# A streaming encoder layer on one core: the threshold searches of the last two tiles are moved from the indexer stage into the attention stage

## The chip, the cores and the metric

The kernel runs on one core of a Trainium2 chip, as one program with no host work between its stages. The metric is device time in microseconds (us) of that core, from start to end of the program. TensorE (PE) does the matmuls, VectorE (DVE), ScalarE (ACT) and GpSimd (POOL) the rest; SyncE (SP) issues the DMAs in one fixed order.

## What is computed

One hybrid layer over a prompt of 4096 positions and a sample of 8 x 16 positions, width 1024. All data are fp32.

```
h = rms_norm(x) ; qa,ka,va,ga, qb,kb,vb,gb, qi,ki,wi = split(h @ w_in)     # 2884 columns
A: 8 heads (2 key heads of 64), window of 128 keys + own chunk of 64, relative bias, sinks
B: score[t,s] = sum_h wi[t,h] * relu(qi[t,h] . ki[s])                      # 4 indexer heads
   keep the 256 highest admissible s for each t (lax.top_k)
   softmax over the kept keys of q.k/8 + bias, 8 heads (2 key heads of 64)
y = x + concat(oA * silu(ga), oB * silu(gb)) @ w_out
```

The kernel does not gather. It finds for each row the value of the 256th highest score, makes a mask of that (0 or -2^100), and B attends densely with the mask added to its scores.

## The kernel before

The prompt is cut into 32 tiles of 128 positions (`TILES`), the sample is tile 32. Tile `t` attends to `(t+1)*128` keys. There are three stages, each a block of its own with its own buffers; a stage starts when every engine has finished the one before.

**Stage one (`stage_one`)** projects, norms and transposes q and k, and scores the indexer for each tile: TensorE's products (L584) go through a relu on ScalarE (L707) and are weighted and added on GpSimd (L876, L878, L881) into a score row; a small memset on GpSimd (L885) marks the row ready. Three row buffers go round. Then each row's threshold is searched: 32 tests (`TESTS`), each a count over the whole row. Even tiles are searched by ScalarE (`search`, L766 and L777, with small steps on L781 and L750 between the tests), odd ones by VectorE (L1009). VectorE closes both kinds: it counts once more for even tiles (L959), then makes the mask with L935, L936, a running sum (L938) and two more passes (L943, L946). SyncE stores the mask to DRAM (`store_chosen`, L421 and L422, tensor `chosen`). An order written out by hand in planned times (`us_at`, `ACT_AT`, `DVE_AT`, `FOUND_AT`, `MASK_AT`) places all other work of ScalarE and VectorE between the tests. Two gate blocks of ten early tiles are projected late, in steps 23 to 32 (`LATER`).

**Stage two (`stage_two`)** does the attention. Each tile has six jobs: `k` = 0, 1 are A (four heads each, two steps), `k` = 2 to 5 are B (two heads each, one step for every 512 keys, so `(t+1)/4` rounded up). TensorE's order in a step is: transpose the exponentiated rows of two heads (`turn`, L1516), apply the step before to the values (`apply`, L1545), then score a unit of a later job (`score`, L1491 for A, L1500 for B). ScalarE copies the transposed block of the first head out of PSUM (L1627), then runs exponentials of a coming job (L1606, up to 1024 keys at once). VectorE copies the second head's block (L1759), then adds mask or bias to the new scores and takes the maximum (L1700). There is one PSUM bank of transposes for each head, so a `turn` waits for the copies of the step before, and two slots of scores.

B's scores are made of split operands in a 32-bit format that TensorE takes in one go (`F32R`): GpSimd makes a rounded part and a remainder of q (L1456, L1458), ScalarE and VectorE do the like for the keys (L1582, L1654), in quarters at the start of tiles 0 to 3. A score unit of 512 keys is then four matmuls, two for each head, with 128 partitions and 512 columns. A's scores (L1491) are plain fp32: 64 partitions, 256 columns, the two key heads in the two halves of the partitions.

At the start of stage two a bias table goes through DRAM (`ramp`, L1414, and `table`, L1418), and the first A job waits for it. **The last stage** projects the output and does the sample.

Of the kernel before, what the change touches and what calls it, by code (L numbers as in the profile page):

```python
# [93 lines left out]
def build(nc, x_prompt, x_sample, cache_a_k, cache_a_v, cache_b_k, cache_b_v, cache_b_kidx,  # L94
          norm_g, w_in, q_norm_a, k_norm_a, q_norm_b, k_norm_b, sink_a, rel_bias, w_out,
          one_hot, eye, outs):
    (y_prompt, y_sample, a_k_prompt, a_v_prompt, b_k_prompt, b_v_prompt, b_kidx_prompt,
     a_k_sample, a_v_sample, b_k_sample, b_v_sample, b_kidx_sample) = outs

    def scratch(name, shape, dt=F32):  # L100
        return nc.dram_tensor(name, shape, dt, kind="Internal").ap()


    qk_t = scratch("qk_t", (TILES + 1, P, T_COLS))
    gates = scratch("gates", (TILES + 1, P, D_MODEL))
# [5 lines left out]
    ramp = scratch("ramp", (P, 2 * HEADS, RAMP))  # L111
    stage_one(nc, x_prompt, x_sample, norm_g, w_in, q_norm_a, k_norm_a, q_norm_b, k_norm_b,
              eye, qk_t, gates, values, chosen, qi_new, ki_new, wi_new,
              a_k_prompt, a_v_prompt, b_k_prompt, b_v_prompt, b_kidx_prompt,
              a_k_sample, a_v_sample, b_k_sample, b_v_sample, b_kidx_sample)
    mixed = scratch("mixed", (TILES, P, D_MODEL))
    stage_two(nc, rel_bias, sink_a, one_hot, eye, qk_t, gates, values, chosen, ramp, mixed, a_k_prompt, a_v_prompt)
    stage_last(nc, x_prompt, x_sample, w_out, mixed, cache_a_k, cache_a_v, cache_b_k, cache_b_v, cache_b_kidx, rel_bias, sink_a, eye,
               qk_t, gates, values, qi_new, ki_new, wi_new, chosen, ramp, y_prompt, y_sample, a_k_sample, a_v_sample)
# [8 lines left out]
TESTS = 32  # L128

# [82 lines left out]
def step_us(t):  # L212

    if t > TILES + 1:
        return 100.0
    a = min(max(t - 2, 2), TILES - 1)
    act = 16 * test_us(a // 2 * 2) + sum(act_us(t, s) for s in range(SLOTS))
    dve = 16 * test_us(a // 2 * 2 + 1) + (close_us(a // 2 * 2) + close_us(a // 2 * 2 + 1)) / 2 + sum(dve_us(t, s) for s in range(SLOTS))
    return max(8.5 * len(groups_of_step(t) if t <= TILES else ()) + 8.0 + 4.0 * len(units(max(t - 1, 0))), act, dve)
# [11 lines left out]
def search_times(first, load, extra):  # L231
# [3 lines left out]
    for a in range(first, TILES, 2):  # L235
# [22 lines left out]
for _a in range(2, TILES):  # L258
# [20 lines left out]
def stage_one(nc, x_prompt, x_sample, norm_g, w_in, q_norm_a, k_norm_a, q_norm_b, k_norm_b,  # L279
              eye, qk_t, gates, values, chosen, qi_new, ki_new, wi_new,  # L280
              a_k_prompt, a_v_prompt, b_k_prompt, b_v_prompt, b_kidx_prompt,
              a_k_sample, a_v_sample, b_k_sample, b_v_sample, b_kidx_sample):
    with ExitStack() as ctx:
# [77 lines left out]
        s_last = sem("sample_stored")  # L361
        s_act = sem("act_ticks")
# [9 lines left out]
        def _(sp):  # L372
# [53 lines left out]
            def chosen_until(us):  # L426

                while stored[0] < TILES and MASK_AT[stored[0]] <= us:
# [78 lines left out]
            sp.wait_ge(s_ch, 16 * 2 * (TILES - 2))  # L507
# [103 lines left out]
        def _(act):  # L611
# [213 lines left out]
            for a in range(2, TILES, 2):  # L825
# [72 lines left out]
        def _(dve):  # L898
# [71 lines left out]
            def background():  # L970

                taken = 2
                for t in range(TILES + 5):
                    for slot in (0, 3, 6, 9, 11):
                        while taken < TILES and FOUND_AT[taken] <= us_at(t, slot):
# [11 lines left out]
                while taken < TILES:  # L987
# [38 lines left out]
            for a in range(3, TILES, 2):  # L1026
# [115 lines left out]
def b_head(k, h):  # L1142

    return 2 * (k - 2) + h
# [115 lines left out]

def exps_of_job(n):
# [9 lines left out]
def stage_two(nc, rel_bias, sink_a, one_hot, eye, qk_t, gates, values, chosen, ramp, mixed, a_k_prompt, a_v_prompt):  # L1271
    with ExitStack() as ctx:
# [9 lines left out]
        kT = sb("kT", [P, KVH, SEQ], F32R)  # L1282
        v = sb("v", [P, TILES, P])
        qa = sb("qa", [P, GROUP, P])
        q_raw = sb("q_raw", [P, HEADS, P])
        q_part = [sb(f"q_part_{i}", [P, 2, HEADS, P], F32R) for i in range(2)]
# [5 lines left out]
        pT = [[sb(f"pT_{h}_{i}", [P, STEP]) for i in range(2)] for h in range(2)]  # L1292
        gate = sb("gate2", [P, D_MODEL])
# [28 lines left out]
        s_khi = sem("keys_rounded")  # L1322
        s_klo = sem("keys_split")
# [3 lines left out]
        s_qr = sem("qb_loaded")  # L1327
# [4 lines left out]
        s_split = sem("q_split")  # L1332
# [16 lines left out]
        s_pool = sem("pool_ticks2")  # L1349
# [3 lines left out]
        def _(sp):  # L1353
# [6 lines left out]
            def load_keys(i):  # L1360

                many = PART // P
                for vh in range(KVH):
                    for half in range(2):
                        sp.dma_start(row[vh][half * HD:(half + 1) * HD, 1, i * PART:(i + 1) * PART].rearrange("p (o n) -> p o n", n=P),
                                     qk_t[i * many:(i + 1) * many, vh * HD:(vh + 1) * HD, 9 * P:10 * P].rearrange("o p n -> p o n")).then_inc(s_kraw[i], 16)
# [6 lines left out]

            sp.wait_ge(s_zero, 1)
# [10 lines left out]
            def load_q(t):  # L1385
                if t:
                    sp.wait_ge(s_split, t)
                for half in range(KVH):
                    rows = slice(half * HD, (half + 1) * HD)
                    sp.dma_start(q_raw[rows, :, :].rearrange("p (v g) n -> p v (g n)", v=KVH),  # L1390
                                 qk_t[t, :, 4 * P:8 * P].rearrange("(v d) n -> d v n", v=KVH)).then_inc(s_qr, 16)
# [9 lines left out]
            def load_mask(t):  # L1401
# [3 lines left out]
                sp.wait_ge(s_near, t - 1)  # L1405
                sp.dma_start(mask[t % 2][:, 0:near], chosen[t, :, 0:near]).then_inc(s_m[t % 2], 16)
# [22 lines left out]
            sp.dma_start(a_v_prompt[0, 0].rearrange("t h d -> t (h d)"), values[TILES - 1, :, 0:P]).then_inc(s_win, 16)  # L1429
            for t in range(TILES + 1):  # L1430
                if t >= 1:
                    sp.wait_ge(s_used, mixed_by(t - 1, 1))
                    sp.dma_start(mixed[t - 1, :, STEP:2 * STEP], mixT[1][:, :]).then_inc(s_store[1], 16)
                if t == TILES:
# [16 lines left out]
        def _(pool):  # L1451
            for t in range(TILES):
                pool.wait_ge(s_qr, 32 * (t + 1))
                if t >= 2:
                    pool.wait_ge(s_unit, units_through(6 * t - 7))
                pool.tensor_copy(q_part[t % 2][:, 0], q_raw[:, :, :]).then_inc(s_pool, 1)  # L1456
                pool.wait_ge(s_pool, t + 1)
                pool.tensor_tensor(q_part[t % 2][:, 1], q_raw[:, :, :], q_part[t % 2][:, 0].bitcast(F32), ALU.subtract).then_inc(s_split, 1)  # L1458
# [12 lines left out]
        def _(pe):  # L1471
# [4 lines left out]
            def score(n, j):  # L1476
# [99 lines left out]
        def _(act):  # L1576
            def round_keys(i):

                act.wait_ge(s_kraw[i], 16 * 2 * KVH)
                cols = slice(i * PART, (i + 1) * PART)  # L1580
                for vh in range(KVH):
                    act.activation(kT[:, vh, cols], row[vh][:, 1, cols], ACT.Copy).then_inc(s_khi, 1)  # L1582

            round_keys(0)

# [29 lines left out]

            for x in PLAN["first"]:
                exponential(*x)
            for n in range(N_JOBS):
                if n % 6 == 0 and 1 <= n // 6 < PARTS:
                    round_keys(n // 6)  # L1620
                for g in range(n_steps(n)):
# [8 lines left out]
                    for kind, m, j in PLACED[n, g]:  # L1630
                        if kind == "gate":
                            copy_gate(m, j)
            copy_gate(TILES - 1, 1)

        @block.vector
        def _(dve):
# [11 lines left out]
            def split_keys(i):  # L1648

                cols = slice(i * PART, (i + 1) * PART)  # L1650
                for vh in range(KVH):
                    dve.wait_ge(s_khi, KVH * i + vh + 1)
                    low = kT[HD:P, vh, cols]
                    dve.tensor_tensor(low, row[vh][HD:P, 1, cols], low.bitcast(F32), ALU.subtract).then_inc(s_klo, 1)  # L1654

            split_keys(0)
# [85 lines left out]

            use(0, 0)
            use(1, 0)
            for n in range(N_JOBS):
                t, k = divmod(n, 6)
                if k == 0 and 1 <= t < PARTS:
                    split_keys(t)
# [4 lines left out]
                for g in range(n_steps(n)):  # L1753
# [592 lines left out]
```

## Time and profile before

| what | value |
|---|---|
| median of 3 runs | 5419.87 us (5418.57 to 5422.72) |
| the profiled execution, its time | 5422.48 us |
| its span, first to last instruction | 5420.7 us |
| PE busy over the span | 4360.3 us (80%), 24457 matmuls |
| DVE busy | 3629.5 us (67%) |
| ACT busy | 3253.0 us (60%) |
| POOL busy | 1729.3 us (32%) |
| mean granted TensorE clock | 0.895 |

The span lies 1.8 us inside the profiled execution's time, and that time is 2.6 us above the median. A busy share is a mean over three stages with different limits, so it has to be read stage by stage. A row of the timeline gives the start in us, the duration, the engine, the line, and how many instructions were merged; what follows an arrow is what ended the wait before it.

### The profile page before, as it was taken

To read this page: it belongs to the slowest core of one execution; us is meant where nothing else is said; L and a number is where in the kernel's file an instruction comes from. 1 tells how busy PE (TensorE), PEld (TensorE's weight loads), DVE (VectorE), ACT (ScalarE), POOL (GpSimd) and SP (SyncE) were. 2 spreads that over 40 slices of the span, in tenths; PEclk is the share of its full clock that TensorE was granted. 3 is DMA by queue.
4 is the path that set the end of the run, shared out by engine and by line. 5 is a ranking of instruction groups with operands and counts; after the bars stand their busy time and mean duration, and the time that the engine had idled before them with its cause. 6 is when DMAs were issued, how large, how long until landed. Compare 5 with 4: busy or idle time off the path is not lost. (4 is left out here: it accounts for less than half of the span.)

```text
span 5420.7 us, 73770 instructions
## 1 busy us (share of the span) xinstructions
PE 4360.3 (80%) x24457; PEld 2782.8 (51%) x24457; DVE 3629.5 (67%) x6737; ACT 3253.0 (60%) x6235; POOL 1729.3 (32%) x1384
## 2 busy tenths in 40 slices
PE   6777777776678777762078899999999999989999
PEld 3434444433334334331046677777777777765454
DVE  2457778888879989898667666666666666635111
ACT  1689788888788789776055555555555555530100
POOL 1454566675758657761022111110000000000000
PEclk9888888888788888886579999999999999999999
DMA  5111111100011011000252111111010100033422
GB/s 133 52 45 41 39 37 38 34 33 33 25 46 39 31 46 38 32 26 31 47 134 71 51 47 43 39 42 43 27 41 28 42 24 28 27 101 121 123 96 99
DMA packets 210852, 280.99 MB, mean 52 GB/s; under 512 B 51200, under 2 KB 139232, under 8 KB 210464
## 3 DMA queue, kind: packets, MB, share of 16 engines
q1 hardware_dynamic: 207520, 276.10, 17.0%
q8 instruction: 204, 3.34, 0.3%
q14 instruction: 168, 1.38, 0.1%
q10 hardware_dynamic: 2960, 0.17, 0.0%
HBM read 165.15 MB, written 112.10 MB: 51 GB/s over the span
## 5 line engine op out<-in xcount | busy, mean ns | idle before, releaser
L1009 DVE TENSOR_SCALAR_CACHE_REDUCE ties<-score,cand 128x512 int8<-128x512 f32 (+14 forms) x480 | 1253.7, 2612 | 141.7 <-POOL score L885 125.3
L568 PE MATMUL bank<-w,x 128*128 128x512 f32 (+1 forms) x2848 | 1241.7, 591 | 25.4 <-DVE w L907 12.6
L777 ACT ACTIVATE act_junk<-score,a_cand,a_sign 128x384 int8<-128x384 f32 (+14 forms) x450 | 990.2, 2201 | 15.0
L1700 DVE CUSTOM_DVE_ANT_0 row<-bank,mask 128x512 f32<-128x512 f32 (+3 forms) x1024 | 623.0, 639 | 465.2 <-PE bank L1500 465.1
L568 PEld LDWEIGHTS bank<-w,x 128*128 128x128 f32 x2848 | 570.0, 204 | 605.1 <-issue 535.0
L1627 ACT ACTIVATE pT<-bank 128x512 f32<-128x512 f32 (+2 forms) x704 | 370.4, 526 | 772.8 <-PE bank L1516 771.9
L584 PE MATMUL bank<-kiT,qi 128*128 128x512 f32 (+3 forms) x1136 | 397.3, 493 | 421.9 <-ACT relu L707 219.7
L1500 PE MATMUL bank<-kT,q_part 128*128 128x512 f32 (+3 forms) x2304 | 658.8, 408 | 11.2 <-DVE part L1700 7.1
L1606 ACT ACTIVATE row<-row,top 128x1024 f32<-128x1024 f32 (+7 forms) x640 | 633.2, 991 | 5.1 <-DVE top L1713 5.0
L1516 PE MATMUL bank<-ident,row 128*128 128x128 f32 x4224 | 574.5, 276 | 52.1 <-DVE pT L1759 48.0
L1545 PE MATMUL bank<-pT,v 128*64 128x128 f32 x8448 | 595.2, 282 | 0.0
L881 POOL TENSOR_TENSOR score<-score,relu 128x512 f32<-128x512 f32 (+3 forms) x426 | 572.8, 1345 | 33.4
L1516 PEld LDWEIGHTS bank<-ident,row 128*128 128x128 f32 x4224 | 497.2, 142 | 134.6 <-DVE pT L1759 54.8
L584 PEld LDWEIGHTS bank<-kiT,qi 128*128 128x128 f32 x1136 | 239.2, 233 | 554.9 <-ACT relu L707 289.6
L878 POOL TENSOR_TENSOR relu<-relu,weight 128x512 f32<-128x512 f32 (+3 forms) x426 | 505.7, 1187 | 0.0
L1545 PEld LDWEIGHTS bank<-pT,v 128*64 128x64 f32 x8448 | 454.4, 137 | 97.7 <-issue 97.4
L1759 DVE COPY pT<-bank 128x512 f32<-128x512 f32 (+2 forms) x704 | 422.9, 601 | 118.0 <-PE bank L1516 116.8
L1456 POOL CAST q_part<-q_raw 128x1024 fp32r<-128x1024 f32 x32 | 33.2, 1038 | 1385.2 <-DMA q_raw<-qk_t 1385.2
L1500 PEld LDWEIGHTS bank<-kT,q_part 128*128 128x128 f32 x2304 | 383.8, 191 | 166.3 <-issue 96.5
L707 ACT ACTIVATE relu<-bank 128x512 f32<-128x512 f32 (+3 forms) x568 | 296.2, 560 | 263.1 <-POOL score L881 177.9
L2102 PE MATMUL bank<-wo,mix_in 128*128 128x512 f32 x1024 | 448.7, 597 | 0.0
L876 POOL TENSOR_TENSOR score<-relu,weight 128x512 f32<-128x512 f32 (+3 forms) x142 | 154.6, 1089 | 765.6 <-issue 553.7
(215 smaller groups left out, 4774.8 us busy)
## 6 DMA issues: line engine op xcount, KB each, us to landing
qk_t<-ring SPq DMA_DIRECT2D x66, 256.0 KB, 2.0
gates<-ring SPq DMA_DIRECT2D x66, 256.0 KB, 2.0
gate<-gates SPq DMA_DIRECT2D x33, 512.0 KB, 3.5
out<-x_in SPq DMA_DIRECT2D x33, 512.0 KB, 2.9
x<-in_x_prompt SPq DMA_DIRECT2D x32, 512.0 KB, 3.7
q_raw<-qk_t SPq DMA_DIRECT2D x64, 256.0 KB, 5.8
mixed<-mixT SPq DMA_DIRECT2D x64, 256.0 KB, 2.1
mix_in<-mixed SPq DMA_DIRECT2D x32, 512.0 KB, 4.3
```

Source lines behind the costliest of these rows:

```text
L568: ins = pe.matmul(p_bank[n % 2][:, 0:n1 - n0], held[:, c * P:(c + 1) * P], w[:, c, n0:n1], start=(c == 0), stop=(c == KC - 1))
L584: ins = pe.matmul(s_bank[at % 4][:, 0:n], qi[:, part, h * P:(h + 1) * P], kiT[:, c:c + n], start=(part == 0), stop=(part == 1))
L777: tick(act.activation(junk, row, ACT.Sign, bias=c, scale=back, accum_out=a_sum[:, :]))
L878: k = tick(pool.tensor_tensor(r, r, weighs, ALU.mult))
L881: pool.tensor_tensor(to, to, r, ALU.add).then_inc(s_pa, 1)
L1009: n = tick(dve.tensor_scalar(ties[:, 0:width], row, c.bitcast(F32), 0.0, ALU.is_ge, ALU.add, accum_out=counts[:, i:i + 1]))
L1500: ins = pe.matmul(s[:, h * STEP:h * STEP + w], q_part[t % 2][:, i, head, :], kT[:, head // GROUP, c:c + w], start=(i == 0), stop=(i == 1))
L1516: ins = pe.transpose(t_bank[h][:, b * P:(b + 1) * P], held, ident[:, :])
L1545: ins = pe.matmul(oT[0 if k < 2 else 1][half * HD:(half + 1) * HD, col:col + P], value, pT[h][at % 2][:, b * P:(b + 1) * P], start=first, ...
L1606: act.activation(at, at, ACT.Exp, bias=bias, accum_out=out).then_inc(s_exp, 1)
L1700: ins = dve.tensor_tensor_reduce(row[k % 2][:, h, c0:c0 + w0], s[:, h * STEP + c0 - c:h * STEP + c0 - c + w0], more, 1.0, PAD, ALU.add, AL ...
L2102: ins = pe.matmul(y_bank[k % 2], held, w[:, c, i * STEP:(i + 1) * STEP], start=(c == 0), stop=(c == KC - 1))
```

## The change

Two things change with it, and a third follows from the room in memory.

1. Stage one searches only tiles 2 to 29 (`SEARCHED` = 30). The finished score rows of tiles 30 and 31 are stored to DRAM (`late`, 128 x 4096 fp32 each, of which 3968 and 4096 columns are used) at the end of SyncE's list, and the stage's end waits for them.
2. Stage two loads row 30 at its start and row 31 at the start of tile 20. ScalarE searches them in pieces placed behind its other work of a B step: 161 pieces over the 208 B steps of tiles 3 to 18, and 161 over the 240 of tiles 20 to 28. VectorE closes them in 23 pieces each, in the B steps of tiles 19 and 29. A test is now four counts over 1024 columns each (the last 896 for tile 30) and one piece of small operations. The masks of tiles 30 and 31 go from a buffer to the mask buffers by DMA.
3. B's scores are no longer split. q and k stay plain fp32 with the two key heads in the two halves of the partitions, a job pairs one head of each half (`b_head`), and a unit of 512 keys is four matmuls of 64 partitions and 256 columns. The casts and subtractions on L1456, L1458, L1582 and L1654 go, and the keys are loaded once (one DMA for a quarter instead of four) and q in one DMA instead of two.

```diff
+SEARCHED = TILES - 2
+LATE_TILES = tuple(range(SEARCHED, TILES))
...
@@ stage_one, sync
+            for a in LATE_TILES:
+                sp.wait_ge(s_sum, a - 1)
+                sp.dma_start(late[a - SEARCHED, :, 0:(a + 1) * P], row_of(a)).then_inc(s_late, 16)
...
+            sp.wait_ge(s_late, 16 * len(LATE_TILES))
@@ stage_one, scalar and vector
-            for a in range(2, TILES, 2):
+            for a in range(2, SEARCHED, 2):
                 search(a)
...
-            for a in range(3, TILES, 2):
+            for a in range(3, SEARCHED, 2):
                 search(a)
@@ the plan of stage two
 def b_head(k, h):
-    return 2 * (k - 2) + h
+    return GROUP + (k - 2 ^ 1) if h else k - 2
...
+QUARTER = 1024
+LATE_SPANS = {1: ((3, 27, 28),), 2: ((3, 18, 19), (20, 28, 29))}[len(LATE_TILES)]
...
+for _a, (_first, _last, _close) in zip(LATE_TILES, LATE_SPANS):
+    _steps, _many = wide_steps(_first, _last), TESTS * (len(quarters(_a)) + 1) + 1
+    for _i in range(_many):
+        LATE_ACT[_steps[_i * len(_steps) // _many]] += 1
+    _steps, _many = wide_steps(_close, _close), 2 + 5 * len(quarters(_a)) + 1
+    for _i in range(_many):
+        LATE_DVE[_steps[_i * len(_steps) // _many]] += 1
@@ stage_two, tensor
-                pe.wait_ge(s_split, t + 1)
-                pe.wait_ge(s_klo, KVH * (t * P // PART + 1))
-                for h in range(2):
-                    head = b_head(k, h)
-                    for i in range(2):
-                        ins = pe.matmul(s[:, h * STEP:h * STEP + w], q_part[t % 2][:, i, head, :], kT[:, head // GROUP, c:c + w],
-                                        start=(i == 0), stop=(i == 1))
+                pe.wait_ge(s_qb[t % 2], 16 * (t // 2 + 1))
+                pe.wait_ge(s_kraw[c // PART], 16)
+                for c0 in range(0, w, 2 * P):
+                    m = min(2 * P, w - c0)
+                    for h in range(2):
+                        vh, g = divmod(b_head(k, h), GROUP)
+                        half = slice(vh * HD, (vh + 1) * HD)
+                        ins = pe.matmul(s[:, h * STEP + c0:h * STEP + c0 + m], qb[t % 2][half, g, :], kT[half, c + c0:c + c0 + m],
+                                        start=True, stop=True)
@@ stage_two, scalar
-            round_keys(0)
...
+                    def count(c, scale):
+                        for q, (c0, n) in enumerate(parts):
+                            act.wait_ge(s_lact, late_tick.n)
+                            late_tick(act.activation(late_junk[:, 0:n], late_row[:, c0:c0 + n], ACT.Sign, bias=c, scale=scale,
+                                                     accum_out=l_sums[:, q:q + 1]))
+                            yield
+                        then(l_sums[:, 4:4 + len(parts)], l_sums[:, 0:len(parts)], ACT.Copy, accum_out=l_sum[:, :])
...
                     for kind, m, j in PLACED[n, g]:
                         if kind == "gate":
                             copy_gate(m, j)
+                    for _ in range(LATE_ACT[n, g]):
+                        next(late_work, None)
@@ stage_two, vector (late_close: the closing passes, in quarters but for the running sum)
+                    m = tick(dve.tensor_tensor_scan(row, tie, tie, 0.0, ALU.add, ALU.max))
...
+                    for _ in range(LATE_DVE[n, g]):
+                        next(late_work, None)
```

## Rows read from the trace of the kernel before

**Rows 1.** Windows by stage: PE, PEld, DVE, ACT, POOL busy, clock, DMA share, GB/s
```profile
0.00:2666.00 2666.00, 1834.40 (x5063) 968.71 (x5063) 2088.40 (x2428) 1998.92 (x3318) 1484.40 (x1278) 0.83 0.13 41
2666.00:2725.00 59.00, 3.53 (x18) 1.91 (x18) 10.09 (x15) 3.65 (x5) 6.82 (x5) 0.50 0.91 165
2725.00:4819.00 2094.00, 1953.31 (x17240) 1531.58 (x17240) 1394.78 (x4018) 1206.32 (x2822) 231.59 (x92) 0.96 0.15 43
```

**Rows 2.** Timeline of VectorE at the end of stage one
```profile
2452.53 4.48 DVE L1009 TENSOR_SCALAR_CACHE_REDUCE ties<-score,cand 128x4096 int8<-128x4096 f32 x1 [18.32 <-POOL score L885]
...
2657.37 4.42 DVE L946 SCALAR_TENSOR_TENSOR mask<-ties,mask 128x4096 bf16<-128x4096 int8 x1
```

**Rows 3.** Timeline of SyncE's DMA queue across the change of stage
```profile
2662.24 0.43 SPq L422 DMA_DIRECT2D chosen<-mask  x1
2666.29 0.34 SPq L1354 DMA_DIRECT2D ident<-in_eye  x1
```

**Rows 4.** GpSimd's groups by line from 2357 to 2453 us; timeline of TensorE
```profile
L876 POOL TENSOR_TENSOR score<-relu,weight 128x512 f32<-128x512 f32 x8 | 8.3, 1039 | 36.9 <-issue 28.9 <-ACT relu L707 8.0
...
2447.35 7.03 PE L568 MATMUL bank<-w,x_later 128*128 128x512 f32 x16
```

**Rows 5.** DMA issues by line: KB each, median us from issue to landing
```profile
ramp<-ramp_sb SPq DMA_DIRECT2D x1, 3064.0 KB, 34.0
...
chosen<-mask SPq DMA_DIRECT2D x1, 960.0 KB, 3.7
```

**Rows 6.** Timeline of TensorE in tile 21: an ordinary step of B
```profile
3817.00 1.09 PE L1545 MATMUL bank<-pT,v 128*64 128x128 f32 x16
3818.02 1.21 PE L1500 MATMUL bank<-kT,q_part 128*128 128x512 f32 x4
3819.07 1.04 PE L1516 MATMUL bank<-ident,row 128*128 128x128 f32 x8
```

**Rows 7.** Timeline of TensorE: an A unit, then parts of it in narrow windows
```profile
3823.65 1.13 PE L1491 MATMUL bank<-ka,qa 64*128 64x256 f32 x8
3824.71 0.98 PE L1500 MATMUL bank<-kT,q_part 128*128 128x384 f32 x4
...
3824.18 0.60 PE L1491 MATMUL bank<-ka,qa 64*128 64x256 f32 x4
...
3824.40 0.38 PE L1491 MATMUL bank<-ka,qa 64*128 64x256 f32 x2
```

**Rows 8.** What TensorE waited for, stage two: total us, times, longest
```profile
PE bank L1516 <- DVE pT L1759: 99.1, 57, 3.6
```

**Rows 9.** Windows of tile 17 and tile 28, columns as in rows 1
```profile
3468.00:3540.00 72.00, 67.98 (x583) 53.35 (x582) 46.64 (x132) 40.81 (x99) 7.51 (x3) 0.93 0.13 39
4407.00:4512.00 105.00, 99.72 (x901) 79.14 (x898) 67.99 (x192) 59.02 (x126) 7.52 (x3) 0.98 0.10 31
```

**Rows 10.** ScalarE's count by forms (min/median/max ns), and two tests of tile 30
```profile
L777 ACT ACTIVATE act_junk<-score,a_cand,a_sign x450: 706/2201/3695, 173.0 to 2520.1; 128x384 int8<-128x384 f32 x10, 128x640 int8<-128x640 f32 x10, 128x896 int8<-128x896 f32 x10, 128x1152 int8<-128x1152 f32 x10
...
2506.01 3.69 ACT L777 ACTIVATE act_junk<-score,a_cand,a_sign 128x3968 int8<-128x3968 f32 x1
2510.58 3.69 ACT L777 ACTIVATE act_junk<-score,a_cand,a_sign 128x3968 int8<-128x3968 f32 x1
```

**Rows 11.** ScalarE's groups by line, stage two: busy us, mean ns, idle before
```profile
L1606 ACT ACTIVATE row<-row,top 128x1024 f32<-128x1024 f32 x416 | 473.8, 1141 | 0.0
L1627 ACT ACTIVATE pT<-bank 128x512 f32<-128x512 f32 x480 | 286.4, 597 | 598.5 <-PE bank L1516 598.3
L1606 ACT ACT_TABLE_LOAD x1 | 1.3, 1283 | 0.0
```

**Rows 12.** VectorE: closing passes of tile 31 (timeline), and stage two's scores
```profile
2644.02 8.69 DVE L938 TENSOR_TENSOR_SCAN score<-ties 128x4096 f32<-128x4096 int8 x1
2652.74 4.48 DVE L943 SCALAR_TENSOR_TENSOR ties<-score,pick,ties 128x4096 int8<-128x4096 f32 x1
...
L1700 DVE CUSTOM_DVE_ANT_0 row<-bank,mask 128x512 f32<-128x512 f32 (+3 forms) x1024 | 623.0, 639 | 465.2 <-PE bank L1500 465.1
```

More of the change, by code:

```diff
@@ L111, in build @@
     ramp = scratch("ramp", (P, 2 * HEADS, RAMP))
+    late = scratch("late", (len(LATE_TILES), P, SEQ))
     stage_one(nc, x_prompt, x_sample, norm_g, w_in, q_norm_a, k_norm_a, q_norm_b, k_norm_b,
-              eye, qk_t, gates, values, chosen, qi_new, ki_new, wi_new,
+              eye, qk_t, gates, values, chosen, late, qi_new, ki_new, wi_new,
               a_k_prompt, a_v_prompt, b_k_prompt, b_v_prompt, b_kidx_prompt,
@@ L116, in build @@
     mixed = scratch("mixed", (TILES, P, D_MODEL))
-    stage_two(nc, rel_bias, sink_a, one_hot, eye, qk_t, gates, values, chosen, ramp, mixed, a_k_prompt, a_v_prompt)
+    stage_two(nc, rel_bias, sink_a, one_hot, eye, qk_t, gates, values, chosen, late, ramp, mixed, a_k_prompt, a_v_prompt)
     stage_last(nc, x_prompt, x_sample, w_out, mixed, cache_a_k, cache_a_v, cache_b_k, cache_b_v, cache_b_kidx, rel_bias, sink_a, eye,
@@ L216, in step_us @@
     a = min(max(t - 2, 2), TILES - 1)
+    both = min(a // 2 * 2 + 1, SEARCHED - 1)
     act = 16 * test_us(a // 2 * 2) + sum(act_us(t, s) for s in range(SLOTS))
-    dve = 16 * test_us(a // 2 * 2 + 1) + (close_us(a // 2 * 2) + close_us(a // 2 * 2 + 1)) / 2 + sum(dve_us(t, s) for s in range(SLOTS))
+    dve = 16 * test_us(both) * (both % 2) + (close_us(a // 2 * 2) + close_us(both)) / 2 + sum(dve_us(t, s) for s in range(SLOTS))
     return max(8.5 * len(groups_of_step(t) if t <= TILES else ()) + 8.0 + 4.0 * len(units(max(t - 1, 0))), act, dve)
@@ L234, in search_times @@
     waiting = sorted(extra)
-    for a in range(first, TILES, 2):
+    for a in range(first, SEARCHED, 2):
         ready = us_at(a + 1, 8.7)
@@ L257 @@
 FOUND_AT, MASK_AT = {}, {}
-for _a in range(2, TILES):
+for _a in range(2, SEARCHED):
     if _a % 2 == 0:
@@ L279, in stage_one @@
 def stage_one(nc, x_prompt, x_sample, norm_g, w_in, q_norm_a, k_norm_a, q_norm_b, k_norm_b,
-              eye, qk_t, gates, values, chosen, qi_new, ki_new, wi_new,
+              eye, qk_t, gates, values, chosen, late, qi_new, ki_new, wi_new,
               a_k_prompt, a_v_prompt, b_k_prompt, b_v_prompt, b_kidx_prompt,
@@ L426, in chosen_until @@
             def chosen_until(us):
-                while stored[0] < TILES and MASK_AT[stored[0]] <= us:
+                while stored[0] < SEARCHED and MASK_AT[stored[0]] <= us:
                     store_chosen(stored[0])
@@ L974, in background @@
                     for slot in (0, 3, 6, 9, 11):
-                        while taken < TILES and FOUND_AT[taken] <= us_at(t, slot):
+                        while taken < SEARCHED and FOUND_AT[taken] <= us_at(t, slot):
                             yield FOUND_AT[taken]
@@ L986, in background @@
                 yield FAR_AWAY - 1
-                while taken < TILES:
+                while taken < SEARCHED:
                     choose_act(taken)
@@ L1258, with wide_steps, quarters @@
             EXP_AT[_x] = len(EXP_AT)
+QUARTER = 1024
+LATE_SPANS = {1: ((3, 27, 28),), 2: ((3, 18, 19), (20, 28, 29))}[len(LATE_TILES)]
+def wide_steps(first, last):
+    return [(n, g) for n in range(6 * first, 6 * last + 6) if n % 6 >= 2 for g in range(n_steps(n))]
+def quarters(a):
+    return [(c, min(QUARTER, (a + 1) * P - c)) for c in range(0, (a + 1) * P, QUARTER)]
+LATE_ACT = {_s: 0 for _s in STEP_AT}
+LATE_DVE = {_s: 0 for _s in STEP_AT}
+for _a, (_first, _last, _close) in zip(LATE_TILES, LATE_SPANS):
[5 more added lines that the diff above has]
+        LATE_DVE[_steps[_i * len(_steps) // _many]] += 1
 def exps_of_job(n):
@@ L1268, in exps_for, with stage_two @@
     return EXP_AT["exp", n, a_place(g, h) if n % 6 < 2 else 2 * (g // 2) + h] + 1
-def stage_two(nc, rel_bias, sink_a, one_hot, eye, qk_t, gates, values, chosen, ramp, mixed, a_k_prompt, a_v_prompt):
+def stage_two(nc, rel_bias, sink_a, one_hot, eye, qk_t, gates, values, chosen, late, ramp, mixed, a_k_prompt, a_v_prompt):
     with ExitStack() as ctx:
@@ L1281, in stage_two @@
         near_bias = sb("near_bias", [P, HEADS, NEAR])
-        kT = sb("kT", [P, KVH, SEQ], F32R)
+        kT = sb("kT", [P, SEQ])
         v = sb("v", [P, TILES, P])
         qa = sb("qa", [P, GROUP, P])
-        q_raw = sb("q_raw", [P, HEADS, P])
-        q_part = [sb(f"q_part_{i}", [P, 2, HEADS, P], F32R) for i in range(2)]
+        qb = [sb(f"qb_{i}", [P, GROUP, P]) for i in range(2)]
         ka = sb("ka", [P, 2, P])
@@ L1326, in stage_two @@
         s_qa = sem("qa_loaded")
-        s_qr = sem("qb_loaded")
+        s_qb = [sem(f"qb_loaded_{i}") for i in range(2)]
         s_ka = sem("ka_loaded")
@@ L1362, in load_keys @@
                 many = PART // P
[L1363 to L1366, printed above, removed]
+                sp.dma_start(kT[:, i * PART:(i + 1) * PART].rearrange("p (o n) -> p o n", n=P),
+                             qk_t[i * many:(i + 1) * many, :, 9 * P:10 * P].rearrange("o p n -> p o n")).then_inc(s_kraw[i], 16)
             def load_part(i):
@@ L1385, in load_q @@
             def load_q(t):
[L1386 to L1391, printed above, removed]
+                if t >= 2:
+                    sp.wait_ge(s_unit, units_through(6 * t - 7))
+                sp.dma_start(qb[t % 2][:, :, :], qk_t[t, :, 4 * P:8 * P].rearrange("p (g n) -> p g n", g=GROUP)).then_inc(s_qb[t % 2], 16)
             def load_values(t):
@@ L1405, in load_mask @@
                 sp.wait_ge(s_near, t - 1)
+                if t in LATE_TILES:
+                    sp.wait_ge(s_lmask, LATE_TILES.index(t) + 1)
+                    sp.dma_start(mask[t % 2][:, 0:near], late_mask[:, 0:near]).then_inc(s_m[t % 2], 16)
+                    sp.dma_start(mask[t % 2][:, near:near + NEAR], late_mask[:, near:near + NEAR]).then_inc(s_m[t % 2], 16)
+                    return
                 sp.dma_start(mask[t % 2][:, 0:near], chosen[t, :, 0:near]).then_inc(s_m[t % 2], 16)
@@ L1429, in _, with load_late @@
             sp.dma_start(a_v_prompt[0, 0].rearrange("t h d -> t (h d)"), values[TILES - 1, :, 0:P]).then_inc(s_win, 16)
+            def load_late(i):
+                if i:
+                    sp.wait_ge(s_lmask, i)
+                width = (LATE_TILES[i] + 1) * P
+                sp.dma_start(late_row[:, 0:width], late[i, :, 0:width]).then_inc(s_lrow, 16)
+            load_late(0)
             for t in range(TILES + 1):
@@ L1433, in _ @@
                     sp.dma_start(mixed[t - 1, :, STEP:2 * STEP], mixT[1][:, :]).then_inc(s_store[1], 16)
+                if t in [close + 1 for _, _, close in LATE_SPANS[:-1]]:
+                    load_late([close + 1 for _, _, close in LATE_SPANS].index(t) + 1)
                 if t == TILES:
@@ L1576, in _ @@
         def _(act):
[L1577 to L1582, printed above, removed]
-            round_keys(0)
             def exponential(kind, n, i):
@@ L1632, in _ @@
                             copy_gate(m, j)
+                    for _ in range(LATE_ACT[n, g]):
+                        next(late_work, None)
+            for _ in late_work:
+                pass
             copy_gate(TILES - 1, 1)
@@ L1646, in _ @@
             dve.tensor_copy(ramp_sb[:, :], bank[0:2 * HEADS, 0:383]).then_inc(s_rampc, 1)
[L1648 to L1656, printed above, removed]
             dve.wait_ge(s_tab, 16 * 2)
```

160 lines of the change are left out of this document (144 added, 16 removed).

## The prediction

> **What bounds the kernel now.** I read the windows by stage first, then the timelines at each stage's end, then a step of stage two. Stage one lasts to 2666 us [rows 1]. At its end only the last search is left: GpSimd has row 31 ready at 2452.5, and from there VectorE counts, closes and is done at 2661.8 [rows 2]; the store goes out at 2662.2 and stage two's first DMA at 2666.3 [rows 3]. So some 210 us of the end are one engine's work on tile 31 (and the closing of tile 30). Then 59 us pass with 3.5 us of matmuls, at a granted clock of 0.50 (the 1.2 GHz level), while the bias table goes through DRAM: the `ramp` DMA alone takes 34.0 us [rows 1, 5]. From 2725 to 4819 TensorE is the bound: 1953 of 2094 us busy, with VectorE at 1395 and ScalarE at 1206 [rows 1]. The last stage, 602 us, is not touched, and I leave it as it is.
>
> **Stage one, removed.** Both searches and both closings of tiles 30 and 31 go, but not all of the time from 2452.5 on is theirs. Row 31 itself stays. Its adds had 8.0 us of waits for ScalarE's relus [rows 4], which were queued behind tests of 3.7 us [rows 10]; those tests are gone, so I put the row at 2444.5. The gates' projections that are still queued on TensorE then, four of 7.0 us [rows 4], start at about 2437 and end at 2465; three transposes, their copies and three stores follow, an estimate of 5 us. SyncE then reaches what is new: two stores of 1984 and 2048 KB, issued together. Their price is not in the trace. A store of 960 KB from the same kind of buffer lands in 3.7 us, which makes 8 us the least for 4032 KB at twice its rate and 15.5 at its own; the `ramp` DMA, 3064 KB in 34.0 us, makes 45 the most [rows 5]. The form is that of the mask store (long rows of one buffer), so I take 12. The stage ends near 2482, stage two starts 1 us later, at 2483.5 instead of 2666.3: **-183 us**, bounds -150 and -190.
>
> **Start of stage two.** The `ramp` chain stays. In front of it in the queue, four key loads become one with half the bytes, and two q loads one: **-3**. Rounding and splitting of the keys at the starts of tiles 1 to 3 goes from ScalarE and VectorE, about 2 us each time (two instructions of 1024 columns, of the size of an exponential [rows 11]): **-6**. GpSimd's q casts lay beside everything; going, they give nothing.
>
> **B's scores.** Before, from the first score matmul of a full unit to the next transpose 1.05 us pass (3818.02 to 3819.07) [rows 6]. After, the unit has the form of half an A unit: eight matmuls of 64 x 256 take 1.06 us (3823.65 to 3824.71) [rows 7]. They run in pairs, one in each half of the partitions: the third pair starts at 3824.18, the fourth at 3824.40, so the pitch is 0.22 us for a pair, the first gap is 0.31 (0.53 less one pitch), and from the last pair to the next instruction it is 0.31 [rows 7]. Two pairs therefore take 0.31 + 0.31 = 0.62 to 0.63, not half of 1.06. I take 0.63, a gain of 0.41; the other end is 0.53, a gain of 0.52. Gaps before the first score matmul are in both forms part of the 1.02 of `apply` [rows 6, 7]. There are 480 full units (ScalarE's 480 copies of 512 columns count the same steps [rows 11]) and 96 partial ones of 128, 256 or 384 keys. Full: 480 x 0.41 = 197. Partial ones cost less before as well (0.98 us for 384 keys against 1.21 for 512 [rows 6, 7]) and have one pair or two after; 0.25 is my estimate of their mean gain, 96 x 0.25 = 24. Together 221.
>
> The Trainium skill, TensorEngine Tiling (Array Packing), section Key Properties, says that tiles run in parallel but that a change of tiling mode drains TensorE. Here the change adds one such switch to a step, since scores used to share the full-array form with the transposes. By the first half alone a unit would take 0.53 and the time would be 5070 (480 x 0.11 less); with the gaps of 0.31 that the row shows, which the second half may be the reason of, it is the sum below. The trace agrees as far as the pitch of the pairs goes.
>
> Not all 221 reach the end. TensorE waited 57 times for VectorE's copy, 99.1 us in all [rows 8]: near an A unit VectorE has several us of work in a row, and what TensorE saves just ahead of it comes back as a longer wait. I take off 0.55 us for each, 31, and 6 for tiles 0 to 7, where steps are few and chains of waits count more. **-184**, bounds -150 (twice the loss) and -245 (0.52 a unit, half the loss).
>
> **The searches on ScalarE.** From 384 to 3968 columns a count grows from 706 to 3695 ns [rows 10], 0.834 ns a column, so 1024 columns take 1.24 us; with the reading of the sum, which overlaps half, 1.25 of the engine. A test's small operations take the rest of 4.57 us between two counts, 0.9 [rows 10], and one more copy with a sum: about 1.2. So 322 pieces of 1.25 are 400 us more on ScalarE, of which 1206 were busy [rows 1]. On average it fits. Tile 17: 72 us less 4 x (4 x 0.41 + 0.27) = 64.4, ScalarE 40.8 + 15.5 x 1.25 = 60.2, 93%. Tile 28: 105 less 12.3 = 92.7, ScalarE 59.0 + 21.5 x 1.25 = 85.9, 93% [rows 9]. But ScalarE is not free evenly. A step of B becomes 3.05 - 0.41 = 2.64 us; ScalarE's copy takes 0.5 of it and an exponential of 1024 columns 1.13 (the rows' durations less the overlap with the next) [rows 11], so a step with one late piece needs 2.9 and one with two exponentials 4.0. The copy may be some 1.4 us late before the next `turn` waits: half a `turn` of 1.04 and 0.6 of copy end it some 1.1 us after the `turn` starts [rows 6, 11], and the next starts at 2.64. Job by job, tile 17: ScalarE 2.4 + 5.5 + 3.9 x 1.25 = 12.8, TensorE 4.5 x 2.64 = 11.9, so 0.9 of a job shows, 3.6 of a tile. In the same way tile 10 has 2.4, tile 28 nothing (18.7 against 19.1). Tiles 3 to 18 at a mean of 2.4 make 39, tiles 20 to 28 some 5, and I add 6 for unevenness: **+50**, bounds +10 (TensorE's present waits of 3 us a tile absorb it) and +130 (0.4 of each piece shows). The wait that takes the place of VectorE's is then "transposes for ScalarE's copy L1627".
>
> **The closings on VectorE.** Its B step is two scores at 0.64 and a copy of like size, 1.9 us [rows 12]; with a quarter of a closing pass, 4.48 / 4 = 1.12 [rows 12], it is over 2.64 by some 0.4, in 12 pieces of a closing (the two cheap passes fit). The running sum is not cut: 8.69 us [rows 12], of which 1.4 are hidden. 12 x 0.4 + 7.3 = 12.1, with small operations 13, twice: **+26**, bounds 15 and 45. What is queued behind it on VectorE is its copy, and TensorE's next `turn` waits for that.
>
> **The reload.** Row 31 (2048 KB) is issued at the start of tile 20 ahead of tile 21's loads, which have a whole tile of time; only ScalarE's first piece may wait, **+3**. Waits that are new on SyncE (for the masks) are long past when it gets there. Row 30's load at the start is queued ahead of tile 2's loads, in place of keys that are no longer loaded twice: 0, at most 5.
>
> **Sum.** -183 - 3 - 6 - 184 + 50 + 26 + 3 = -297. The profiled execution's 5422.5 less 297 is 5125.5; it stood 2.6 above the median, so 5123.
>
> **The rivals.**
> - ScalarE binds more than I think: lateness does not heal between jobs, because late pieces stand ahead of the copy for which TensorE waits. At the upper bound, +130, the time is 5203. For it: 93% mean use in both tiles, and exponentials in pairs. Against: TensorE already waits 3 us in each tile.
> - The scores gain nothing: the pairs do not overlap in this place, or the switches eat it. Then -184 goes, and ScalarE has its old 3.05 us step, which saves about 30 of the 50: 5277. Against it stand the A units, which are in the same place of the step.
> - Everything hides and the unit costs 0.53: -245 instead of -184, +10 and +15 instead of +50 and +26, near 5010.
> - Slower: ScalarE has to change its function tables between the searches' sign and the exponentials. Stage two has one table load of 1283 ns now, before its first exponential [rows 11], and that exponential and copy share a table is all that it shows. With a load before and after each of 322 pieces, 826 us are added; ScalarE then has 1206 + 400 + 826 = 2432 us of work in a stage of 2094, and the time is at least 5423 - 183 - 9 + 338 = 5569, with stalls some 5650. It decides from about 115 pieces with a pair of loads, all of them exposed (297 / 2.57). The Trainium skill, ScalarE: Activation LUTs, section on table sets, speaks of this danger (batch calls by set) and prices a switch at 2.66 us, by which it would be twice as bad; it also says that cheap functions are in every set. No row here has sign beside an exponential.
>
> **How the numbers follow.** The sum as taken, within 60 us: 0.60. ScalarE binds: 0.18. Scores gain nothing: 0.07. All hides: 0.11. Tables: 0.04. The range runs from 5030 to 5220: it takes in the likeliest case, the first rival, and the upper bound of the late rows' stores, and leaves out most of the other three. A difference of 0.2% (11 us) is what a measurement of this kernel can tell from none. Only the tables make it slower: faster 0.95, the same 0.01, slower 0.04.
>
> **What would show it.** Stage two's first DMA near 2484; stage one's last wait of SyncE for the stores of late rows, some 12 us. In an ordinary step of a tile without late work (tile 30 or 31) a period of 2.64 instead of 3.05, and score units of four matmuls of 64 x 256 in 0.63. In tiles 3 to 18 waits of L1516 for ScalarE's copy, 2 to 4 us a tile. In tiles 19 and 29 one gap of 7 us behind the running sum. One table load in stage two. The prediction is wrong if the unit takes 0.8 or more, if the waits for ScalarE's copy add up to over 100 us, or if the rows' stores take 30.

## The result, and the profile after

The changed kernel takes 5289.19 us (median of 4 runs, 5285.59 to 5291.09) against 5420.36 before (4 runs): a ratio of 0.9757, 95% interval 0.974 to 0.9774, so 131 us less. The forecast was 5123. The profiled execution has a span of 5286.3 us.

First the windows by stage of the kernel after, columns as in [rows 1]:

```profile
0.00:2481.00 2481.00, 1828.35 (x5063) 968.10 (x5063) 1884.68 (x2277) 1858.14 (x3170) 1485.85 (x1278) 0.86 0.14 45
2481.00:2538.00 57.00, 3.53 (x18) 1.91 (x18) 7.09 (x13) 1.79 (x4) 3.35 (x39) 0.50 0.88 162
2538.00:4687.00 2149.00, 1988.78 (x19288) 1491.53 (x19288) 1445.42 (x4077) 1559.40 (x3622) 127.49 (x31) 0.97 0.12 39
```

Stage one ends 185 us sooner, as forecast. But stage two, which should have lost some 110 us (-184 - 6 + 50 + 26 + 3), has become 55 longer (2149 after 2094), and TensorE is busier in it than before (1988.8 after 1953.3), with 19288 entries after 17240. ScalarE has 353 us more to do there, and that is not where the time went, as TensorE's waits show (total, times, longest):

```profile
PE bank L1577 <- DVE pT L1935: 117.5, 63, 7.3
PE bank L1577 <- ACT pT L1756: 16.8, 35, 1.0
```

It waits 16.8 us in all for ScalarE's copy, and 18 us longer than before for VectorE's [rows 8]. The end of stage one, in SyncE's DMA queue:

```profile
2469.23 0.94 SPq L508 DMA_DIRECT2D late<-score  x2
2481.07 0.34 SPq L1403 DMA_DIRECT2D ident<-in_eye  x1
```

The late rows go out at 2469.2 and stage two's first DMA at 2481.1. So the two stores hold the end of the stage for 12 us, as the forecast took it.

Now an ordinary step of B in tile 17, TensorE's timeline, to be set beside [rows 6]:

```profile
3305.79 1.13 PE L1561 MATMUL bank<-kT,qb 64*128 64x256 f32 x8
3306.86 1.09 PE L1577 MATMUL bank<-ident,row 128*128 128x128 f32 x8
3307.88 1.09 PE L1606 MATMUL bank<-pT,v 128*64 128x128 f32 x16
3308.90 1.13 PE L1561 MATMUL bank<-kT,qb 64*128 64x256 f32 x8
```

The score unit of 512 keys has eight entries, not four, and takes 1.07 us (3305.79 to 3306.86), where the old one took 1.05. The whole step is 3.11 us (3305.79 to 3308.90) against 3.02 (the score unit before the one in [rows 6] starts at 3815.00, that one at 3818.02). The forecast had 0.63 and 2.64. The unit is in every respect what an A unit is in [rows 7], and this is the clue. In the code both have four matmuls. By source line, with number of entries and min/median/max in ns:

```profile
L1561 PE MATMUL bank<-kT,qb x4352: 269/376/793, 2539.1 to 4651.7; 64*128 64x256 f32 x184, 64*128 64x128 f32 x14
```

The program issues 480 x 4 + 32 x (4 + 2 + 2) = 2176 of these matmuls, and the trace has 4352. A plain fp32 matmul is two entries. The old ones, in the split format, were one entry each: 2304 in the profile's page for 576 units of four.

Two windows by tile, for tiles 17 and 28, to be set beside [rows 9]:

```profile
3283.00:3356.00 73.00, 68.50 (x657) 51.28 (x656) 47.05 (x133) 57.78 (x137) 4.09 (x1) 0.95 0.11 35
4255.00:4361.00 106.00, 100.66 (x1012) 75.71 (x1012) 68.33 (x192) 83.03 (x182) 4.09 (x1) 1.00 0.09 28
```

ScalarE has 17 and 24 us more to do in these tiles, and they are 1 us longer each.

### The profile page after: what moved, and what is told of

Same layout as the page of the kernel before. It is cut to its first block and busy times, and to the rows that moved or that the text cites. A ratio compares the mean times of both kernels' runs of the same rounds, so it can differ in the third digit from the quotient of the medians.

```text
span 5286.3 us, 78323 instructions
## 1 busy us (share of the span) xinstructions
PE 4389.2 (83%) x26505; PEld 2741.8 (52%) x26505; DVE 3473.8 (66%) x6644; ACT 3463.7 (66%) x6887; POOL 1623.2 (31%) x1358
## 5 line engine op out<-in xcount | busy, mean ns | idle before, releaser
L1018 DVE TENSOR_SCALAR_CACHE_REDUCE ties<-score,cand 128x512 int8<-128x512 f32 (+13 forms) x448 | 1110.6, 2479 | 122.4 <-POOL score L894 107.1
L786 ACT ACTIVATE act_junk<-score,a_cand,a_sign 128x384 int8<-128x384 f32 (+13 forms) x420 | 879.8, 2095 | 14.0
L1526 POOL TENSOR_TENSOR near_bias<-table,mask 128x2048 f32<-128x2048 f32 (+1 forms) x32 | 129.6, 4050 | 1932.3 <-DVE part L1824 1879.6
L1577 PE MATMUL bank<-ident,row 128*128 128x128 f32 x4224 | 603.2, 283 | 69.5 <-DVE pT L1935 65.4
L1561 PE MATMUL bank<-kT,qb 64*128 64x256 f32 (+1 forms) x4352 | 615.6, 399 | 14.6 <-DVE row_a L1798 7.4
L1577 PEld LDWEIGHTS bank<-ident,row 128*128 128x128 f32 x4224 | 455.6, 142 | 256.2 <-issue 168.6
L1606 PEld LDWEIGHTS bank<-pT,v 128*64 128x64 f32 x8448 | 458.2, 138 | 97.8 <-issue 97.4
L1561 PEld LDWEIGHTS bank<-kT,qb 64*128 64x128 f32 x4352 | 383.1, 189 | 136.6 <-issue 82.5
```

The source lines that it names most:

```text
L786: tick(act.activation(junk, row, ACT.Sign, bias=c, scale=back, accum_out=a_sum[:, :]))
L1018: n = tick(dve.tensor_scalar(ties[:, 0:width], row, c.bitcast(F32), 0.0, ALU.is_ge, ALU.add, accum_out=counts[:, i:i + 1]))
L1561: ins = pe.matmul(s[:, h * STEP + c0:h * STEP + c0 + m], qb[t % 2][half, g, :], kT[half, c + c0:c + c0 + m], start=True, stop=True)
L1577: ins = pe.transpose(t_bank[h][:, b * P:(b + 1) * P], held, ident[:, :])
L1606: ins = pe.matmul(oT[0 if k < 2 else 1][half * HD:(half + 1) * HD, col:col + P], value, pT[h][at % 2][:, b * P:(b + 1) * P], start=first, ...
```

## Experiments

Theory 1: the score unit is no quicker, since its count of matmuls was misread, and is even 0.09 us of a step slower; the late work costs little. Theory 2, the rival: the unit is quicker somewhere, and the late pieces on ScalarE eat what it gains.

**Each part alone.** The first kernel has the new scoring and no late search; the second has the late rows stored and loaded, but neither searched nor closed; the third has ScalarE's pieces and no closings. The second and third leave out the masks of tiles 30 and 31 (all zero), so they give times only.

```diff
@@ first kernel
-SEARCHED = TILES - 2
+SEARCHED = TILES
...
@@ second kernel
-                    for _ in range(LATE_ACT[n, g]):
-                        next(late_work, None)
...
@@ second and third kernel
-                    for _ in range(LATE_DVE[n, g]):
-                        next(late_work, None)
```

> The changed scoring and nothing else: all searches are back in stage one, no late row is stored, loaded or searched. Theory 1 (the new score unit is no quicker: a plain fp32 matmul of the code is two entries of the trace, so an A unit's eight entries are the four matmuls of a whole new unit): a B step is 3.11 us instead of 3.02, 480 steps cost some 43 us, the keys' splitting and the shorter start give back 15, so about 5448. Theory 2 (the unit gains 0.41 as forecast and ScalarE's late pieces eat it in the changed kernel): about 5420 - 184 - 9 = 5227.

> The changed kernel without the pieces on ScalarE and VectorE: the late rows are stored and loaded, never searched or closed, and the masks of tiles 30 and 31 are all zero. Theory 1: stage two loses only the closings, 30 us, and little else: about 5255. Theory 2 (the pieces hide a gain of the scores): about 5289 - 184 - 30 = 5075.

> The changed kernel with ScalarE's 322 pieces, without VectorE's 46 closing pieces (the masks of tiles 30 and 31 are all zero). Against the run without any late work it gives the price of ScalarE's pieces, against the changed kernel that of the closings. Theory 1: closings 29 us, so 5260, and ScalarE's pieces 5 or less, since a step of 3.11 us has room for 2.9. Theory 2: ScalarE's pieces cost over 100 us, closings 29: 5260 too, but then the run without late work is at 5160 or below.

Measured: scores alone 5450.5 against 5420.8 for the kernel before, timed beside it (ratio 1.0054, 1.0037 to 1.007); no late work 5258.7; no closings 5261.1. Theory 1 had 5448, 5255 and 5260. The new scoring makes the kernel slower by itself, by 30 us net of what the keys' splitting gives back. ScalarE's 322 pieces cost 5261.1 - 5258.7 = 2.4 us, less than the scatter of two runs: with the same code in stage one, stage two's first DMA went out at 2477.4 in the second kernel and at 2481.1 in the changed one. VectorE's closings cost 5289.2 - 5261.1 = 28. Theory 2 falls with the first kernel.

**Are the halves used side by side?** The heads of a job are paired as before, so both lie in the same half of the partitions.

```diff
-    return GROUP + (k - 2 ^ 1) if h else k - 2
+    return 2 * (k - 2) + h
```

> The changed kernel with the heads of a job paired as before (both in one half of the partitions), so that no two score matmuls can run side by side. Theory 1: the side-by-side pairs are what keeps the new unit at 1.06 us; without them it takes about 8 x 0.22 + 0.1 = 1.9, and 528 units of 512 keys cost some 440 us more: about 5730. A rival, that the halves do not overlap in this place and the unit is merely cheap, gives no change: 5289.

5652.2 us. TensorE's timeline:

```profile
3503.83 1.99 PE L1561 MATMUL bank<-kT,qb 64*128 64x256 f32 x8
3505.75 1.09 PE L1577 MATMUL bank<-ident,row 128*128 128x128 f32 x8
```

The unit now takes 1.92 us, 0.85 more, so two halves do run side by side in the changed kernel. Full units make 480 x 0.85 = 408 (there are 480, not the 528 of the expectation); 363 arrive. TensorE's waits for VectorE's copy account for 52 us of the difference, since they fall from 117.5 to:

```profile
PE bank L1577 <- DVE pT L1935: 65.2, 55, 6.4
```

That is more than the 45 missing, and the 96 partial units, which must cost more as well, are not in the 408; the rest was not taken apart.

**The form of the unit.** One matmul of 512 columns for each head instead of two of 256, and in another kernel the unit ahead of `apply`.

```diff
-                for c0 in range(0, w, 2 * P):
-                    m = min(2 * P, w - c0)
+                for c0 in range(0, w, 4 * P):
+                    m = min(4 * P, w - c0)
```

> The changed kernel with one matmul of 512 columns for each head of a score unit instead of two of 256. Theory: the unit is bound by the streaming of its columns, in two entries of the trace for each matmul, side by side in two halves, and by a gap of 0.31 us at either end. The columns stay the same, only the first gap can hide behind a longer first matmul: 0.0 to 0.1 us less in 480 steps, 5240 to 5289. A rival, that the number of instructions sets the unit: half the entries, 0.5 us a unit, near 5040.

```diff
                     turn(n, g)
+                    if last is not None and [kind for kind, _, _ in PLACED[n, g]] == ["score"]:
+                        score(*PLACED[n, g][0][1:])
+                        apply(*last)
+                        last = (n, g)
+                        continue
```

> The changed kernel with the score unit of a step in front of the applying of the step before, where a step has one unit and no gate. The number of changes between full-array, halved and column-split matmuls stays three for a step. Theory: 3.11 us of a step against 3.02 come from the entry into and out of the halved form (gaps of 0.31 and 0.17 us beside 0.23 and 0.11), whatever stands next to it: the same, 5280 to 5300; VectorE gets its scores a microsecond earlier, which may take some of the 117 us of waits for its copy.

5290.1 and 5292.8 us: no change in either that stands out from the scatter of the runs. In the first a unit is

```profile
3507.74 1.13 PE L1561 MATMUL bank<-kT,qb 64*128 64x512 f32 x4
3508.80 1.09 PE L1577 MATMUL bank<-ident,row 128*128 128x128 f32 x8
```

1.06 us with half the entries, so the number of matmuls is not what it costs; the columns are, as the half units below confirm. The order of the parts does not matter either.

**If the unit had been what the forecast took it for.** From tile 6 on the second half of each wide unit is left out (its scores are those of an earlier unit), which leaves two pairs of entries side by side, with the late work and, as in the second kernel, without.

```diff
-                for c0 in range(0, w, 2 * P):
+                for c0 in range(0, w if t < 6 else 2 * P, 2 * P):
```

> The changed kernel with the second half of each wide score unit left out from tile 6 on (its scores are those of an earlier unit), so that a unit is two pairs side by side, the form that the forecast priced at 0.63 us. It tests the rest of the forecast. By its steps: 468 x 0.43 + 7 - 31 = 177 less, and with a step of 2.68 us the late pieces on ScalarE cost 50 and not 2: 5289 - 177 + 48 = 5160. If ScalarE still hides all: 5112. If ScalarE binds (0.4 of each piece): 5240.

> The same half units without any late work on ScalarE and VectorE (as in the second experiment; masks of tiles 30 and 31 zero). By the forecast's steps 5259 - 177 = 5082; the run before less this one is the price of the late work at the shorter step, forecast as 76 (50 and 26).

5136.2 and 5097.8 us. The first kernel's step, where the unit takes 0.63 us as the forecast had it for a unit of this size:

```profile
3513.84 0.70 PE L1561 MATMUL bank<-kT,qb 64*128 64x256 f32 x4
3514.47 1.09 PE L1577 MATMUL bank<-ident,row 128*128 128x128 f32 x8
```

Half the unit gives back 153 us with the late work and 161 (5258.7 - 5097.8) without, where the forecast's way of counting gave 177. The late work costs 38 at the shorter step (5136.2 - 5097.8), not the 76 forecast and not the 30 of the longer step (5289.2 - 5258.7). TensorE's waits here:

```profile
PE bank L1577 <- DVE pT L1935: 140.2, 68, 7.7
PE bank L1577 <- ACT pT L1756: 23.8, 44, 2.8
```

Even with a step of 2.68 us ScalarE does not bind. The same two waits in the kernel without late work are 119.0 and 14.3 us, so the late work adds 21 us of waits for VectorE and 10 for ScalarE. The shorter step itself adds 21 for VectorE (97.8 to 119.0, both without late work), which the forecast took at 31. With 21 in place of 31 its count would be 187, and 161 arrive; the missing 26 were not taken apart. The granted clock over stage two is 0.95 without late work at the short step and 0.97 at the long one, which has that sign.

**Two versions that should be faster.** A closing's running sum is cut into eight pieces, and row 30's closing lies over tiles 18 and 19 (ScalarE's pieces then end with tile 17).

```diff
-                    m = tick(dve.tensor_tensor_scan(row, tie, tie, 0.0, ALU.add, ALU.max))
+                    for c in range(0, width, EIGHTH):
+                        n = min(EIGHTH, width - c)
+                        tie = late_tie[:, c:c + n]
+                        dve.wait_ge(s_dve, tick.n)
+                        tick(dve.tensor_tensor_scan(late_row[:, c:c + n], tie, tie, late_row[:, c - 1:c] if c else 0.0, ALU.add, ALU.max))
+                        if c + n < width:
+                            yield
```

> The changed kernel with the running sum of a closing cut into eight pieces of 512 columns that hand the sum on, and row 30's closing spread over tiles 18 and 19 instead of 19 alone. Theory: the closings cost 28 us because one instruction of 8.4 us stands in front of VectorE's copy, and pieces of 1.1 us fill what the step leaves; cut, 18 of the 28 us go: 5271. A rival, that the closing costs by its sum of work on VectorE: no change, 5289, since the work stays the same.

5270.9 us (0.9719, 0.9705 to 0.9734), as expected. The 18 us are the gain of both edits, which were not run apart. What the cut removes is seen in the changed kernel in tile 19, first VectorE, then TensorE:

```profile
3478.54 8.42 DVE L1902 TENSOR_TENSOR_SCAN late_row<-late_tie 128x3968 f32<-128x3968 int8 x1
...
3487.13 0.68 DVE L1935 COPY pT<-bank 128x512 f32<-128x512 f32 x1
```

```profile
3480.17 0.66 PE L1577 MATMUL bank<-ident,row 128*128 128x128 f32 x4
3487.87 1.11 PE L1577 MATMUL bank<-ident,row 128*128 128x128 f32 x4 [7.05 <-DVE pT L1935]
```

The sum takes 8.42 us, the copy behind it starts at 3487.1, and TensorE stands for 7.05; in tile 29 it is 8.69 and 7.31. With the cut sum the longest wait is 3.7 us, and all waits for VectorE's copy make 105.0 us instead of 117.5.

In the other version the late rows are stored inside step 32 of SyncE's list, and the last kernel has both.

```diff
                     from_ring(ki_new, HD, P)
+                    for a in LATE_TILES:
+                        sp.wait_ge(s_sum, a - 1)
+                        sp.dma_start(late[a - SEARCHED, :, 0:(a + 1) * P], row_of(a)).then_inc(s_late, 16)
```

> The changed kernel with the stores of the two late rows issued in step 32, behind the sample's indexer operands, and not at the end of SyncE's list. The 11 us from their issue to stage two's first DMA are then behind the last gates' projections. Theory: 9 us less, 5280. A rival: row 31 is ready too late and its wait holds up the stores behind it: 0 or slower.

> The changed kernel with both, the running sum in pieces and the early stores. They are in different stages and should add: 5289 - 18 - 9 = 5262.

5284.3 us (0.9743, 0.9727 to 0.9759) for the early stores, 5259.8 (0.9702, 0.9687 to 0.9717) for both. In the profiled execution of the early stores stage two starts 12 us sooner (first DMA at 2468.6, not 2481.1), of which 3 were there before the moved stores (the gates' store ahead of them goes out at 2441.7, not 2444.7); the other 9 are what was expected. But the median moved by 5, less than its runs differ (5278.1 to 5288.8). With identical instructions from there on, its tiles 20 to 22 took 6.7 us longer at a granted clock of 0.94 to 0.96 than in the changed kernel at 0.96 to 0.98. So that gain is not shown in the time by itself. The version with both is 29 us below the changed kernel and the best of those that leave nothing out; it is 11 below the cut sum alone, though the runs of the two overlap (5253.8 to 5267.8, and 5264.5 to 5272.3).

## Why the prediction was wrong

It failed at one step, **B's scores**, "the unit has the form of half an A unit: eight matmuls of 64 x 256 take 1.06 us". The row says x8, and the code beside it, two times two matmuls, says four. Each plain fp32 matmul is two entries of the trace, so an A unit is a whole new unit, and [rows 7] already said what a new one costs: 1.06 us from its start to the next instruction, against 1.05. I counted entries on one side (eight for A) and matmuls of the code on the other (four for the new unit). The unit took 1.07 us, over the 0.8 that the prediction named as the sign of being wrong, and the whole gain of 184 was missing. The bounds of the step, 0.63 and 0.53, rested on the same reading, so the range left out 1.06. The other rows gave warning too: `apply` has four blocks for two heads, eight matmuls, and stands as x16.

Term by term, forecast and measured:

- Stage one: -183, and -185 (2666.3 to 2481.1). The two stores held it for 12, as taken. The row of tile 31 was ready at 2450.5, not 2444.5, and the gates' projections were done at about 2462, not 2465; the row was not what the end waited for.
- Start and splitting of keys: -9, and -14 (3.8 up to the end of tile 0, 9.9 in tiles 1 and 2 together, by VectorE's last product of each tile).
- Scores: -184. Alone they cost 29.7 us net, so with the 14 above +43, which is 480 x 0.09. (The step before was 3.02, not the 3.05 of the prediction.) Of the 0.09, 0.02 to 0.03 are in the unit and 0.06 in the transposes behind it (1.02 us for eight, where the kernel before has 0.96, 3819.07 to 3820.03). Starts inside the units show where. The new unit's pairs start 0.32, 0.22 and 0.21 us after one another, and 0.32 pass from the last to the transposes; the old unit's matmuls were 0.34, 0.24, 0.24 and 0.23 apart. So the new form streams a little faster and has a gap of 0.1 at its end that the old one had not, and the first transpose behind it is 0.16 ahead of the second, not 0.11. Where a B unit follows an A unit, in the same form, the gap between them is gone:

```profile
3744.80 1.13 PE L1550 MATMUL bank<-ka,qa 64*128 64x256 f32 x8
3745.77 1.03 PE L1561 MATMUL bank<-kT,qb 64*128 64x256 f32 x8
3746.73 1.10 PE L1577 MATMUL bank<-ident,row 128*128 128x128 f32 x8
```

  The A unit takes 0.97 us here against 1.06 in [rows 7], where a full-array unit follows, and the B unit 0.96 against 1.07. With the unit moved, the transposes stand behind `apply`, which is another form too, and still take 1.02 (3509.71 to 3510.73). So the loss goes with the change between forms of matmul; what TensorE does in these gaps no row shows. The Trainium skill, TensorEngine Tiling (Array Packing), section Key Properties, says that changing the tiling mode drains TensorE; the rows agree with its sign, and with its statement that tiles run in parallel (1.07 us against 1.92).
- Searches on ScalarE: +50, and 2.4. At the real step of 3.11 us there is room for the 2.9 that a step with a piece needs. At 2.68 us the whole late work costs 38 and adds 10 us of waits for ScalarE's copy, so the term would have been some 10 (an estimate) and was too high: I let lateness add up over jobs. That it heals in the A jobs is likely and not shown.
- Closings: +26, and 28. Reload: +3, and 2.7, ScalarE's one wait for the row, which is part of the pieces' 2.4 above.

These make -126 of the 131 measured (-185 - 14 + 43 + 2 + 28).

Of the rivals, "the scores gain nothing" is what happened, at 5277 forecast and 5289 measured, with a chance of 0.07. It was the right outcome for another reason: the pairs do overlap, and there are twice as many. The rival of function tables did not come: stage two has a single table load, as before [rows 11], with sign and exponential in turns all through tiles 3 to 28. ScalarE did not bind: the waits for its copy add up to 16.8 us, where the prediction named 100 as the sign.

## What to carry to other kernels

Before a group of the trace is used as the price of new code, divide its count by the count in the code: an entry is not a matmul, and formats differ in how many entries and passes they make. Work for an engine with idle time cost next to nothing here (2.4 us for 322 pieces), since each piece was smaller than what a step leaves, even at 78% use of that engine; one undivided instruction of 8 us in front of a copy that the bound engine waits for cost almost all of its length (7.05 of 8.42). A part of a change that makes room for another (here the plain keys, which free the buffers that the late row needs) should be priced alone, since it can cost what nobody looks for: the scoring cost 30 us. By difference the searches' move alone is worth 161, but no kernel was run that moves them and keeps the split scores.

## What the runs showed of the hardware

A plain fp32 matmul appears as two entries. At a granted clock of 1.00 (the 2.4 GHz level) an entry of 256 columns takes 0.21 to 0.22 us, which is two cycles a column, also where nothing runs beside it (eight entries in the same half take 1.92 us, with a gap of 0.3 at each end). So the matmul costs four cycles a column, and two halves side by side bring it to two; the split format did two matmuls of one entry at 0.24 us for 512 columns and came to about the same. A unit in halves has a gap of about 0.1 us at each side where another form stands, and none where another unit in halves does (0.96 against 1.07 us with one such side less). Sign, relu, identity, copy and exponential ran in turns on ScalarE with one table load of 1283 ns in the whole stage. ScalarE's count over 1024 columns took 1.23 us, where [rows 10] had given 1.24.
